# Router logits from turned x and a one-hot product for the first expert block, in a two-layer mixture-of-experts kernel

## What is computed

```python
x = x + gt_a * (o @ w_o[i])
hf = _modulate(_rmsnorm(x, g_ffn[i]), sh_f, sc_f)      # h * (1 + scale) + shift
...
y = _hier_moe(tokens, w_group[i], b_group[i], w_router[i], b_router[i], w_gate[i], w_up[i], w_down[i])
x = x + gt_f * y
...
def _hier_moe(h, ...):
    p_grp = softmax(h @ w_group + b_group)             # 4 groups, the best is taken
    lg = h @ w_router + b_router                       # 32 experts, 8 of them in the group
    ...                                                # the two best of the group
    y = (silu(xe @ w_gate[e]) * (xe @ w_up[e])) @ w_down[e]
    ...                                                # weighted sum per token
```

## Time and profile before

| what | before |
| --- | --- |
| median of three runs | 2111.34 us (2108.47 to 2114.01) |
| profiled execution | 2110.83 us |
| its span in the trace | 2109.0 us |
| PE busy | 1971.9 us, 93% |
| VectorE busy | 1062.7 us, 50% |
| ScalarE busy | 405.5 us, 19% |
| GpSimd busy | 118.9 us, 6% |
| mean DMA rate | 277 GB/s |
| mean granted clock | 0.976 |

### The profile page before, as it was taken

One profiled execution on the slowest core, in us unless ns is written; L12 is line 12 of the kernel. 1 busy time (PEld: TensorE's weight loads), 2 busy tenths in 40 slices (PEclk: granted clock), 3 DMA queues, 4 the chain that ended last, 5 costly groups with the idle time before them and its releaser, 6 DMA issues.

```text
span 2109.0 us, 20648 instructions
## 1 busy us (share of the span) xinstructions
PE 1971.9 (93%) x8057; PEld 888.9 (42%) x8057; DVE 1062.7 (50%) x1974; ACT 405.5 (19%) x836; POOL 118.9 (6%) x168
## 2 busy tenths in 40 slices
PE   6999987999999999988799988898999999999999
PEld 2445443333333333454333333333445554445554
DVE  1257545445554445674433222322767665666665
ACT  2146411000000002162100000000312230212230
POOL 1001002000000000000100000000100000100000
PEclk9999997999999999999799999999999999999999
DMA  9267435999999998455599999999733333723431
GB/s 356 98 232 264 184 127 223 416 425 426 427 427 427 426 427 329 173 210 188 220 425 426 427 425 427 425 426 424 268 114 120 120 120 120 255 101 115 140 134 65
DMA packets 95043, 584.23 MB, mean 277 GB/s; under 512 B 10044, under 2 KB 14436, under 8 KB 62044
## 3 DMA queue, kind: packets, MB, share of 16 engines
q1 hardware_dynamic: 84400, 559.96, 65.7%
q0 software_dynamic: 10256, 21.86, 3.1%
q10 hardware_dynamic: 288, 1.05, 0.2%
HBM read 589.05 MB, written 4.26 MB: 281 GB/s over the span
## 4 chain that ended last, share of the span: by engine, by line
PE 76%; DMA 13%; DVE 8%; ACT 2%; SPq 1%; issue 1%; DVEq 0%; POOLq 0%; ACTq 0%
PE bank L816 25%; PE bank L1144 11%; PE bank L821 6%; DMA ring<-in_w_gate 6%; PE bank L975 6%; DMA ring<-in_w_up 4%; PE bank L1223 4%; PE bank L1159 3%; PE bank L1120 3%; PE bank L1043 2%; PE bank L766 2%; PE bank L663 2%; PE bank L754 2%; PE bank L804 1%; DMA ring<-in_w_qkv 1%
## 5 line engine op out<-in xcount | busy, mean ns | idle before, releaser
L816 PE MATMUL bank<-ring,big 128*64 128x512 f32 x2464 | 684.7, 602 | 25.7 <-DMA ring<-in_w_gate 10.0
L816 PEld LDWEIGHTS bank<-ring,big 128*64 128x64 f32 x2464 | 217.7, 138 | 387.3 <-issue 374.2
L2165 DVE TENSOR_TENSOR big<-bank,big 128x512 f32<-128x512 f32 x192 | 131.6, 685 | 252.3 <-PE bank L821 251.5
L816 PE MATMUL bank<-big 128*64 128x512 f32 x512 | 227.5, 594 | 0.0
L1144 PE MATMUL bank<-ring,big 128*128 128x512 f32 (+1 forms) x448 | 205.3, 600 | 5.3 <-DVE ring L2548 3.3
L821 PE MATMUL bank<-big 128*128 128x512 f32 x360 | 180.1, 610 | 0.0
L975 PE MATMUL bank<-ring,big 128*128 128x512 f32 x320 | 141.8, 602 | 3.8 <-ACT big L1435 2.0
L1144 PEld LDWEIGHTS bank<-ring,big 128*128 128x128 f32 x448 | 82.6, 193 | 93.9 <-issue 92.8
L2369 DVE TENSOR_TENSOR big<-big,bank 128x512 f32<-128x512 f32 x32 | 22.0, 687 | 184.5 <-PE bank L816 184.5
L975 PEld LDWEIGHTS bank<-ring,big 128*128 128x128 f32 x320 | 61.2, 193 | 80.0 <-issue 74.7
L816 PEld LDWEIGHTS bank<-big 128*64 128x64 f32 x512 | 68.6, 137 | 58.9 <-issue 58.9
(11 more groups left out here) (443 smaller groups left out, 2380.8 us busy)
## 6 DMA issues: line engine op xcount, KB each, us to landing
ring<-in_w_gate SPq DMA_DIRECT2D x52, 2048.0 KB, 17.9
ring<-in_w_up SPq DMA_DIRECT2D x51, 2048.0 KB, 21.2
ring<-in_w_down SPq DMA_DIRECT2D x51, 2048.0 KB, 20.5
ring<-in_w_ada SPq DMA_DIRECT2D x24, 2048.0 KB, 10.4
ring<-in_w_in SPq DMA_DIRECT2D x24, 2048.0 KB, 7.9
big<-in_w_up SPq DMA_DIRECT2D x9, 2048.0 KB, 21.3
big<-in_w_down SPq DMA_DIRECT2D x9, 2048.0 KB, 21.6
big<-in_w_gate SPq DMA_DIRECT2D x8, 2048.0 KB, 19.2
```

Of the source, the lines that this page charges most:

```text
L816: ins = nc.tensor.matmul(bank[half * CAP:(half + 1) * CAP, :], lhs[:, k, half * CAP:(half + 1) * CAP], slot_cols(slots[half], k * step + c ...
L2165: return r, V.tensor_tensor(r, bank, GATE[tile // LAT][:, half * 512:(half + 1) * 512], ALU.mult)
```

## The change

There are two parts, both in both layers (`DEALT = (0, 1)`).

**Router logits from turned x.** Instead of turning the modulated rows, PE turns the rows of x as soon as they are updated (`x_turn`, two halves, both emptied by ScalarE). The scale is put into the router weights (`WRM[s] = WRT * (1 + scale) * g_ffn`, one for each stream), rstd is applied as VectorE takes the logits in `route`, and the shift becomes a bias row (`BRM = shift @ WRT + BRT`). For this the shift and scale of each stream and g_ffn are loaded as rows of 128 (`MROWS`), turned by PE (`columns_turn`), multiplied with the router weights (`shift_product`) and spread to all partitions (`shift_rows`). PE waits on `s_pre` for all the loads, VG's included. The modulated rows are still made, in four buffers, since experts and store need them; those of the last tile get their shift (`shifted_rows`) only after the last `route`. The order of the steps around the tiles is written anew.

**Block 0 by a one-hot product.** `first_slots` makes for every tile a matrix `OHF` of tokens by the 128 slots of block 0; PE multiplies `Hf` with it and sums over the tiles, which gives the turned rows of block 0 in PSUM. GpSimd no longer clears and gathers block 0, and PE no longer turns it.

```diff
-        Hf = [cut(13824 + D * i, D) for i in range(2)]
+        Hf = [cut(a, D) for a in (13824, 14848, 17920, 20480)]
...
+                def columns_turn():
+                    pe.wait_ge(s_pre, due(s_pre, 16 * (2 + streams)))
+                    n = 16 * streams + KD
+                    nc.tensor.transpose(unit("A")[:, 0:n], MROWS[0:n, :], ident[0:n, 0:n]).then_inc(s_unitA, 1)
...
+                def shift_product():
+                    pe.wait_ge(s_outA, count["A"])
+                    u = unit("A")
+                    for k in range(KD):
+                        ins = nc.tensor.matmul(u[0:36, 0:streams], WRT[:, k, :], MCOL[:, k:k + 16 * streams:16], start=(k == 0), stop=(k == KD - 1))
...
+                def x_turn(tile, half):
+                    u = unit("A")
+                    for k in range(4):
+                        c = (4 * half + k) * P
+                        ins = nc.tensor.transpose(u[:, k * P:(k + 1) * P], X(tile)[:, c:c + P], ident)
...
-                    wo_part(u, tile, 0, range(KD)).then_inc(s_unitD, 1)
...
+                    if tile == 0:
+                        wo_part(u, tile, 0, range(4))
+                        columns_turn()
+                        wo_part(u, tile, 0, range(4, KD)).then_inc(s_unitD, 1)
+                        shift_product()
+                    else:
+                        wo_part(u, tile, 0, range(2))
+                        pe.wait_ge(s_xr, X_BEFORE + tile)
+                        x_turn(tile - 1, 0)
+                        x_turn(tile - 1, 1)
+                        wo_part(u, tile, 0, range(2, 6))
+                        logits(tile - 1)
+                        wo_part(u, tile, 0, range(6, KD)).then_inc(s_unitD, 1)
...
+                logits(tiles - 1, 0)
+                pe.wait_ge(s_xr, X_BEFORE + tiles)
+                x_turn(tiles - 1, 1)
+                logits(tiles - 1, 1)
...
+                if layer in DEALT:
+                    pe.wait_ge(s_h, h_rows)
+                    pe.wait_ge(s_oh, due(s_oh))
+                    for k in range(KD):
+                        for tile in range(tiles):
+                            ins = nc.tensor.matmul(banks[k // 4][:, (k % 4) * P:(k % 4 + 1) * P],
+                                                   Hf[tile].rearrange("p (n k) -> p k n", k=KD)[:, k, :], OHF[:, tile, :],
+                                                   start=(tile == 0), stop=(tile == tiles - 1))
+                    ins.then_inc(expert_sems[layer][1], 1)
                 slot_map(layer, BATCHES[layer][1], False, True)
...
+                act.wait_ge(s_mod, (128, 256)[layer])
+                for s in range(streams):
+                    act.dma_start(MROWS[16 * s:16 * s + 16, :], mod_d[layer, s, 3 * D:5 * D].rearrange("(k p) -> k p", p=P)).then_inc(s_pre, 16)
+                act.dma_start(MROWS[16 * streams:16 * streams + KD, :], t["g_ffn"][layer].rearrange("(k p) -> k p", p=P)).then_inc(s_pre, 16)
                 act.dma_start(VG, t["g_ffn"][layer].partition_broadcast(P)).then_inc(s_pre, 16)
...
+                route(layer, *BATCHES[layer][1])
+                shifted_rows(layer, tiles - 1)
...
+                if layer in DEALT:
+                    first_slots(*BATCHES[layer][1]).then_inc(s_oh, one(s_oh))
                 map_rows(*BATCHES[layer][1])
+                if layer in DEALT:
+                    dve.wait_ge(s_xt, 1)
+                    V.tensor_copy(XT[0][:, 4:8, :], banks[1][:, :].rearrange("p (k n) -> p k n", k=4)).then_inc(s_xtD, 1)
                 map_out(0, PAIRS)
```

More of the change, by code:

```diff
@@ L581, in batch_ending @@
             return None
+        DEALT = (0, 1)
         marks = {}
@@ L883, in overflow @@
                     pe.wait_ge(o_ct, units * OV[layer] + 1)
-                pe.wait_ge(s_xe[0], 16)
-                turns(0).then_inc(s_xt, 1)
+                if layer not in DEALT:
+                    pe.wait_ge(s_xe[0], 16)
+                    turns(0).then_inc(s_xt, 1)
                 for b in range(PAIRS):
@@ L908, in experts @@
                     if b + 1 < PAIRS:
-                        pe.wait_ge(s_xe[1 - j], 16 * ((b + 1) // 2 + 1))
+                        pe.wait_ge(s_xe[1 - j], 16 * ((b + 1) // 2 + (0 if j and layer in DEALT else 1)))
                         if layer == 0 and b >= 2:
@@ L1047, in logits @@
+                X_BEFORE = (NT, 3 * NT)[layer]
+                def logits(tile, half=None):
                     a, b = [x for x in BATCHES[layer] if x[0] <= tile < x[1]][0]
-                    if tile == a:
+                    if tile == a and half != 1:
                         pe.wait_ge(s_psd, so_far(s_ps))
-                    pe.wait_ge(s_outA, turned[tile][0])
-                    pe.wait_ge(s_outD, turned[tile][1])
-                    for k in range(KD):
-                        ins = nc.tensor.matmul(banks[6][:, (tile - a) * 36:(tile - a) * 36 + 36], hT(tile, k), WRT[:, k, :],
+                    pe.wait_ge(s_outA, turned[2 * tile + (0 if half == 0 else 1)])
+                    for k in range(KD) if half is None else range(4 * half, 4 * half + 4):
+                        ins = nc.tensor.matmul(banks[6][:, (tile - a) * 36:(tile - a) * 36 + 36], hT(tile, k), WRM[tile // LAT][:, k, :],
@@ L1054, in logits @@
                                                start=(k == 0), stop=(k == KD - 1))
-                    if tile == b - 1:
+                    if tile == b - 1 and half != 0:
                         ins.then_inc(s_lg, 1)
@@ new lines, in _ @@
+                    if final:
+                        release(n0, "D")
+                    u = unit("D")
+                    wo_part(u, tile, 1, range(4))
+                    if tile == 0:
+                        shift_rows()
+                    if final:
+                        pe.wait_ge(s_xh, layer + 1)
+                        x_turn(tile, 0)
+                    wo_part(u, tile, 1, range(4, 7))
+                    if final and batch_ending(layer, tiles - 2):
+                        positions(*batch_ending(layer, tiles - 2))
@@ L1437, in modulated_to_ht, with rows_to_ht @@
                     ins.then_inc(s_outA, 1)
-            def rows_to_ht(tiles):
-                for tile in tiles:
-                    u = take()
-                    copy_out(HT[:, 0:4, tile * P:(tile + 1) * P], u[:, :].rearrange("p (k n) -> p k n", k=4))
+            def rows_to_ht(tile, half):
+                u = take()
+                copy_out(HT[:, 4 * half:4 * half + 4, tile * P:(tile + 1) * P], u[:, :].rearrange("p (k n) -> p k n", k=4))
             act.wait_ge(s_x, 16)
@@ L1996, in route @@
                 dve.wait_ge(s_lg, due(s_lg))
-                V.tensor_tensor(lg, banks[6][:, 0:36 * n].rearrange("p (t e) -> p t e", t=n), bc(BRT.unsqueeze(1), P, n, 36),
-                                ALU.add).then_inc(s_v, one(s_v))
+                for tile in range(a, b):
+                    bias = BRM[:, 36 * (tile // LAT):36 * (tile // LAT) + 36]
+                    ins = V.scalar_tensor_tensor(LG[:, tile, :], banks[6][:, 36 * (tile - a):36 * (tile - a) + 36], rstd[:, tile:tile + 1], bias,
+                                                 ALU.mult, ALU.add)
+                ins.then_inc(s_v, one(s_v))
                 dve.wait_ge(s_v, so_far(s_v))
@@ L2074, in map_rows, with first_slots @@
                 ins.then_inc(s_oh, one(s_oh))
+            def first_slots(a, b):
+                for tile in range(a, b):
+                    V.tensor_scalar(OHF[:, tile, :], C("iota"), DST[:, tile, 0:1], None, ALU.is_equal).then_inc(s_v, one(s_v))
+                dve.wait_ge(s_v, so_far(s_v))
+                for tile in range(a, b):
+                    ins = V.scalar_tensor_tensor(OHF[:, tile, :], C("iota"), DST[:, tile, 1:2], OHF[:, tile, :], ALU.is_equal, ALU.add)
+                return ins
             def map_out(a, b):
@@ L2270, in out_part @@
                     dve.wait_ge(s_outD, so_far(s_outD))
-                    done = s_v if c == 0 else s_xr
+                    done = s_xr if c else s_xh if tile == tiles - 1 else s_v
                     V.tensor_tensor(X(tile)[:, cs], X(tile)[:, cs], RES, ALU.add).then_inc(done, one(done))
@@ L2929, in _ @@
                 pool.wait_ge(s_lg, 2 * (layer + 1))
-                zeroed(0)
+                if layer not in DEALT:
+                    zeroed(0)
                 zeroed(1)
@@ L2935, in _ @@
                 pool.wait_ge(s_map, 2 * layer + 1)
-                gather(0)
+                if layer not in DEALT:
+                    gather(0)
                 gather(1)
```

143 lines of the change are left out of this document (90 added, 53 removed).

## The result

| what | before | changed |
| --- | --- | --- |
| median | 2114.99 us (2108.47 to 2116.79, 8 runs) | 2118.63 us (2117.96 to 2122.93, 8 runs) |
| profiled execution, its span | 2110.83, 2109.0 us | 2118.79, 2116.9 us |
| PE busy | 1971.9 us | 1987.6 us |

The ratio is 1.0026 with a 95% interval of 1.0016 to 1.0036: the change costs 5.5 us (3.4 to 7.6). I had forecast a gain of 3.2 us and a range up to 2113, so the direction and the time were both wrong. (The ratio is estimated from all the runs; the two medians of the table are 3.6 us apart, inside that interval.) The later runs of the kernel before are 3.6 us above the three that I had; that moved the time, but not the direction.

A forecast was written before the change was run, and what follows sets the result against it. PE bounds it (93% busy), with layer 1's expert blocks DMA-bound. Layer gains of -9.5 and -10.6 us (-20.1) plus +16.9 for VG's wait gave -3.2, so 2108.1 us; range 2093 to 2113, its own 2103 to 2112.

The forecast's parts named there:

- The stall: Output product, after four steps: PE waits 6.45 and 6.05 us for VG, plus 2.2 us each at half clock; +16.9 us.
- Rival A: VG lands as early as before, stalls only 2.45 and 2.0 us, clock stays up; 2095.7 us, chance 0.30.
- B: VG lands late, but the clock stays high or drops late; 2103.7 us, chance 0.12.
- C: The queue ahead of VG is drained first, stalls of 8.8 and 13.9 us; 2118.4 us, chance 0.06.
- The tail: From the last unit's end or scaled rows to the last routing: shorter by 7.2 us in layer 0, 8.4 in layer 1.
- From the output product to the last routing: Whole piece from output product to last routing, stall included: +1.15 us in layer 0, +1.65 in layer 1.
- The one-hot product: Block 0's product replacing the gather, priced at 0.111 us per warm pass: 9.7 us in layer 0, 6.1 in layer 1.
- The clock inside the product: PE starts block 0's one-hot product cold; full clock back 5.1 us in, after 23 cold passes.
- D: The one-hot product stays cold to its end and the first blocks' warm gain goes; 2117.9 us, chance 0.04.
- The one-hots: VectorE making the token-by-slot matrices before the product: 1.0 us for four operations in layer 0, 0.5 in layer 1.
- The first block: Block 0 starts with PE already warmed by the one-hot product: -2.7 us in layer 0, -1.6 in layer 1.
- The rule that block 0 carries all behind it: Both layers: whatever moves block 0 moves the rest of the program by the same amount, also in DMA-bound layer 1.

The follow-up runs named there:

- consecutive weights: Changed kernel with block 0's one-hot product reading 128 consecutive numbers as weights instead of every eighth, computing wrong numbers; ratio to before 0.9994.
- VG on its own semaphore: Changed kernel with VG's load raising a semaphore only VectorE waits for, TensorE waiting for the small row loads alone; ratio to before 0.9970.
- VG first: Changed kernel with ScalarE issuing VG's load ahead of the row loads, TensorE still waiting for all of them; ratio to before 1.0005.
- both edits and the later turn: Changed kernel with VG's separate semaphore, modulated rows written in TensorE's reading order, and the columns turned six steps later; ratios to before 0.9933 and 0.9921.

## Why the prediction failed, step by step

**The stall was right.** The wait was where I put it, after four steps, behind the same load, with 6.05 and 7.33 us where I had 6.45 and 6.05. Rival A, that VG lands in 4.5, fell; it does so only when issued ahead of w_up. The clock fell during the gap in both layers and was still down behind it, which rules out B; the four steps behind the gap took 1.6 and 2.1 us more than at full clock, where I had 2.2 each:

```profile
249.00:250.00 1.00, 1.00 (x3) 0.45 (x2) 0.00 (x0) 0.00 (x0) 0.00 (x0) 0.50 0.08 16
...
982.00:983.00 1.00, 1.00 (x2) 0.45 (x2) 0.00 (x0) 0.00 (x0) 0.00 (x0) 0.50 1.01 426
```
C needed 8.8 and 13.9 us; the real gaps are far below.

**The tail was right to a microsecond or two.** From the output product to the last routing I had +1.15 and +1.65 and it was +0.68 and +3.13; the longer stall of layer 1 is 1.3 of the miss of 1.5 there. That is no luck of two errors: from the end of the last unit to routing, layer 0 took 12.33 us before and 5.14 now, -7.2 as forecast. One detail was not: in layer 0 routing waited 0.26 us for PE's second half of the logits and not for the scaled rows.

**The one-hot product failed.** The step was "the nearest row is a warm 128 x 128 product with new weights each time ... 0.111 us each". That row reads its weights in a row; the product reads every eighth number, and the line of code says so. I took a price from a row that agreed in shape and type but not in access. The term was 9.7 and 6.1 us; measured 15.51 and 7.88, and 9.57 and 5.44 once the stride is taken away. The clock inside the product did rise about as forecast, 4.7 us after its start (0.95 in the window from 333 to 334), but the strided loads did not get faster with it. The 5.8 and 1.8 us are 7.6 of the 11 us between forecast and profile. D, "the product stays cold", came close to the slower time (2117.9) for a wrong reason: the window from 338 to 340 above is at full clock, and the product is as slow there.

**The one-hots** were sized too small: 1.85 us for the four operations of layer 0 where I had 1.0.

**The first block stayed partly cold.** I had -2.7 in layer 0 for a warm start, and it was -1.0, because the clock went down again in block 0. PE's only gap shortly before is one of 0.48 us, which the kernel with consecutive weights has too, where the clock stays up. A window shows it (stretch, length, busy by engine, PEclk, DMA share, GB/s):

```profile
348.00:350.00 2.00, 2.00 (x8) 0.65 (x6) 1.79 (x7) 0.50 (x1) 2.00 (x4) 0.50 0.70 201
```

It belongs neither to the stride nor to the kernel: it is there in the changed kernel and with VG on its own semaphore, not with VG first, which has the stride too (the first 33 passes in 7.51 us, as at full clock), and of the two profiles of the kernel with both edits and the later turn one has it and one has not, as shown above. So 1.7 of this term is left to the execution, and why it goes one way or the other stays open. In layer 1 I had -1.6, measured -1.57.

**The rule that block 0 carries all behind it held:** in layer 0 the turns of block 1 are 6.55 us later and those of the last block 6.5; in layer 1, where the DMAs bound the blocks, it is 6.85 and 6.7.

## What to carry to other kernels

Before you take a price from the nearest row, compare the access pattern too: here a float32 operand with 32 bytes from one number to the next cost 1.75 times in the weight loads of a product at full clock, nearly nothing in them at half clock, and 1.6 times in VectorE. A wait placed early for a small load can be long when a large load was issued just ahead of it (6.1 us for 4 KB here); give each load its own semaphore, wait for the smallest set, and put the wait as late as the work allows. And when one part of a change makes something late that another part no longer needs, measure the parts separately before you keep both: here half of the one-hot product bought nothing.

## What the runs showed of the hardware

**The granted clock goes down while PE works, at places that differ between executions.** Windows of three kernels over attention of layer 1, whose code they share: before, changed, and VG on its own semaphore.

```profile
822.00:825.00 3.00, 2.67 (x10) 2.15 (x11) 2.30 (x8) 2.19 (x6) 0.00 (x0) 0.50 1.02 399
```

```profile
822.00:825.00 3.00, 3.00 (x26) 0.67 (x24) 2.69 (x7) 1.45 (x3) 0.00 (x0) 1.00 1.04 401
...
904.00:909.00 5.00, 3.48 (x16) 2.20 (x20) 1.54 (x4) 0.35 (x1) 0.00 (x0) 0.50 1.05 401
```

```profile
829.00:834.00 5.00, 4.41 (x12) 2.86 (x13) 3.96 (x10) 2.45 (x7) 0.00 (x0) 0.50 1.03 399
...
908.00:912.00 4.00, 3.17 (x15) 1.51 (x17) 1.30 (x2) 0.00 (x0) 0.00 (x0) 0.50 1.05 393
```

The changed kernel has one such stretch at half clock there, the other two have two; before, the first is over by 825 (0.96 from 825 to 828), with VG on its own semaphore it lasts from 829 to 834 and more. The part between the last turns of layer 0 and the output product of layer 1 is 191.9 us in the changed kernel, 192.3 before and 195.0 with VG on its own semaphore. All twelve profiles go with this: without a stretch near 825 the part takes 191.6 to 192.3 us (six profiles), with three windows of 1 us at 0.50 there 192.3 to 194.3 (three profiles), and with six such windows 195.0 to 195.3 (three profiles). So one such stretch can be some 3 us, as much as the effects that this study tries to tell apart. Why a stretch appears in one execution and not in another is open; no run here was made for it. It is one more reason to compare the two lengths, and medians of many runs, and not the spans of single profiles.

**A small load is not quick.** 4 KB issued 0.36 us behind a 2 MB load took 6.1 us to be there (239.14 to 245.21), and 7.5 us as the fourth behind VG. Issued 0.13 us ahead of the 2 MB load, the same rows were in at 976.30 at the latest, 3.2 us after their issue. Whether the order of issue alone decides for such rows, or what else moves at the time, no run separates.
